# First 62 up-projection units as one 448-column product and one 224-column product

## The chip, the cores and the metric

The kernel runs on one core of one Trainium2 chip. The metric is device time in microseconds, the median of several executions. One execution was also taken with the profiler, and all rows below are of that one.

## The reference, cut to what matters

The reference is a two-layer transformer block over 256 tokens of width 1024: attention and a gated recurrence, then a feed-forward of 16384 experts chosen by keys (PEER), then a second block with a mixer, cross attention and a gated MLP. Everything is fp32. The part that matters here is the expert layer:

```python
sc = jnp.einsum('bshpd,phnd->bshpn', q, keys)     # scores; top 16 of 2 x 128 keys for each of 8 heads
act = jax.nn.gelu(jnp.einsum('tkd,td->tk', ue, ht), approximate=False)   # up-projection of the chosen experts
return jnp.einsum('tk,tkd->td', gt * act, ve)     # gated, down-projection
```

The kernel computes the up-projection of all 16384 experts for 224 of the tokens (the dense part), masks with gates later, and gathers the experts of the other 32 tokens.

## The kernel before, in words

**fp32 in three products.** TensorE's products here are of float32r, so each operand is split into a high part and a low rest: ScalarE makes the high half of a weight unit (`hi`, raw to `whi`), VectorE or GpSimd the low one (`lo`, `wlo = raw - whi`), and `three` adds high x high, high x low and low x high into one PSUM region. A unit is 128 x 1024 weights, 512 KB, fetched by SyncE into 4 `raw` buffers; `whi` and `wlo` have 3 buffers each. The tokens, transposed, stand in `hTh` (high) and `hTl` (low), 8 tiles of 256 columns each.

**The up-projection** (L1075 to L1080) is 128 units, each with 8 steps over k. In one step `lin_T` runs three products of 224 columns, with three weight loads: `whi` on `hTh`, `whi` on `hTl`, `wlo` on `hTh`. Two units share one PSUM bank (224 columns in each half); the banks 4, 5 and 6 go round, the bank being 4 + pair mod 3. After each pair ScalarE applies gelu straight from PSUM into `acts` (L1607 to L1614) and frees the bank.

**Beside it**, in the first 62 units, runs the routing of the tokens (L2045), in two blocks of 128 tokens, nearly all on VectorE. It is a generator of 30 steps. Each engine's program is written by hand: per unit it does its own share and then `side.step`, which runs one step of the routing, or two where `U1_STEPS` (L162) says so: after units 12, 26, 40 and 54. `side.drain` after unit 61 runs what is left. In VectorE's part of a block the steps 1 to 10 are the top 16 of 16 score rows of 128, step 11 casts and adds the candidates, 12 to 21 the top 16 of them, 22 the positions, 23 to 26 comparisons and sums that look up the keys, 27 waits for ScalarE's exponential (its step 22) and normalizes, 28 and 29 are empty, and 30 (L2096 to L2115) waits for three transposes that TensorE makes in its step 30, and copies them out.

**Who makes the low halves.** `on_pool` (L133) gives those that are made in iterations 0 to 51 to GpSimd and the later ones to VectorE. In iteration u an engine prepares unit u + 2. A high half waits until the unit three before it is done on TensorE.

**The gathered tokens.** In iteration 51 VectorE scales one row block (L2124), ScalarE copies it three times in iterations 52 to 54, GpSimd gathers expert rows from iteration 50 on, and VectorE's dot products (L2131) come at iterations 55, 56, 58, 59, 61 and later.

After unit 61 the remaining 66 units run with `lin_T` as well; from unit 70 on the gates are built beside them.

Of the kernel before, what the change touches and what calls it, by code (L numbers as in the profile page):

```python
# [7 lines left out]
ALU = mybir.AluOpType  # L8
# [11 lines left out]
T = 256  # L20
# [14 lines left out]
NG = 32  # L35
# [3 lines left out]
NGRP = TD // OB  # L39
EARLY = 10  # L40
G_DENSE = 70
REP_AT = 51
DOT_AT = [55 + 3 * g // 2 for g in range(EARLY)] + [71 + 2 * (14 * g // 11) for g in range(NPK - EARLY)]
ACC_AT = [57 + 2 * g for g in range(13)] + [97 + 3 * g // 2 for g in range(NPK - 13)]
# [125 lines left out]
hd_pe hd_act hd_dve hd_pool mask xv_ev cr_pe cr_act cr_dve  # L170
ff_a ff_c ff_g ff_h ff_lo
own_act own_dve own_pool zeros x_sq hi_half lo_half lo_first f_xg f_xd f_act hd_mask
pk_idx pk_rep pk_used pk_act
""".split()


# [37 lines left out]
def build(nc, x, mem, wdram, keep_d, con0_d, con1_d, con2_d, keys_d, w2c_d, gf_d, gf2_d,  # L214
          gffn_d, utab, out):
    ctx = ExitStack()
    with ctx:
        def sb(name, n, dt=F32, c=ctx):
            return c.enter_context(nc.sbuf_tensor(name, [P, n], dt))
# [7 lines left out]
        wlo = [sb(f"wlo{i}", UNIT, F32R) for i in range(NSPL)]  # L227
        keep = sb("keep", NKEEP)
        xres = sb("xres", 2048)
        hTh = sb("hTh", 2048, F32R)  # L230
        hTl = sb("hTl", 2048, F32R)
        small = sb("small", 256)
        with ExitStack() as c:
            iT = sb("iT", 3 * T, c=c)
# [6 lines left out]
        row_b = sb("row_b", T, F16)  # L241
        col_b = sb("col_b", T, F16)
        iota_b = sb("iota_b", P * 2, F16)
        zero_b = sb("zero_b", P, BF16)
        first_cut = (sb("first_h", 2 * T, F32R), sb("first_l", 2 * T, F32R))

        with ExitStack() as c:
            A1 = sb("A1", 24576, c=c)
# [23 lines left out]
        def t3(ap, a):  # L272
            return ap.rearrange("p (a b) -> p a b", a=a)

        def t4(ap, a, b):
            return ap.rearrange("p (a b c) -> p a b c", a=a, b=b)
# [18 lines left out]

        K_ = pick(keep, 0, KOFF)
        ident = K_("ident")
        hTv = (t3(hTh[:, :], KD), t3(hTl[:, :], KD))
        xk_end = BASE["w_xk"]

        aqT = t3(a1(0, 1280), 5)
# [64 lines left out]
        acts = t3(A2[:, 0:P * TD], P)  # L366
        hrep = a2(31744, 1024)
        pk_acc = hrep
        pk_idx = small[:, 16:16 + NPK].bitcast(U32)
        pk_gate, pk_dot, pk_co, pk_f = (small[:, o:o + NPK] for o in (48, 80, 112, 144))  # L370

# [8 lines left out]

        def cut(part, n):
            if n < 2:
                return t3(first_cut[part][:, :], 2)[:, n, :]
            return t3((hTh, hTl)[part][:, :], 8)[:, n % 8, :]


        memx = a3(0, 2048)
# [67 lines left out]
        def pe_program(e):  # L455
# [132 lines left out]

            def normed(j):
                return lambda k: e.wait_ge(s["n_lo"], 8 * j + 2 * (k // 2) + 2) if k % 2 == 0 else None  # L590

            def lin_T(u0, units, src, K, first=None, after=None, steps=(1,), c0=0):
                per = KD // K
                for u in range(units):
                    i = u0 + u
                    wv = [z.rearrange("p (n k c) -> p n k c", n=per, k=K) for z in unit(i)]
                    for j in range(per):
                        n = u * per + j
                        q = pair[0]
                        bk = 4 + q % 3  # L600
                        if n % 2 == 0:
                            use(bk)
                        for k in range(K):
                            if n == 0 and first:
                                first(k)
                            ins = three(banks[bk][:, (n % 2) * 256:(n % 2 + 1) * 256 - c0], [z[:, j, k, :] for z in wv],
                                        [z[:, k, c0:T] for z in src], k == 0, k == K - 1)
                            if 2 * (j * K + k + 1) == KD:
                                mid.step()
                        if n % 2:  # L610
                            by, n_ev = PAIR_FREED[q]
                            free[bk] = (s[by], n_ev)
                            pair[0] += 1
                    ins.then_inc(s["w"], 1)
                    if after:
                        after(u)
                    side.step(steps[(i + 1) % len(steps)])
# [455 lines left out]
                    ins.then_inc(s["sc_pe"], 1)  # L1073
                    free[g] = (s["sc_act"], 4 * b + g + 1)
            side.lists[0] += [routing(0), routing(1)]  # L1075
            lin_T(BASE["u"], 62, hTv, KD, steps=U1_STEPS, c0=NG)
            side.drain()
            lin_T(BASE["u"] + 62, G_DENSE - 62, hTv, KD, c0=NG)
            side.lists[0] += [gates(0), gates(1)]
# [107 lines left out]
        def act_program(e):  # L1187
# [57 lines left out]
            def lin_T(u0, units, evict, after=None, per=1, steps=(1,)):  # L1245
                for u in range(units):
                    i = u0 + u
                    hi(i + 2)
                    if (u + 1) * per % 2 == 0:
                        q = pair[0]  # L1250
                        e.wait_ge(s["w"], i + 1)
                        evict((u + 1) * per - 2, t3(banks[4 + q % 3][:, :], 2))
                        pair[0] += 1
                    if after:
                        after(u)
                    side.step(steps[(i + 1) % len(steps)])
# [350 lines left out]
            def gelu(n0):  # L1607
                def f(n, pb):
                    if TD * (n0 + n + 2) > 15872:
                        e.wait_ge(s["rt_dve"], 8)  # L1610
                    if TD * (n0 + n + 2) > 16896:
                        e.wait_ge(s["pk_used"], EARLY)
                    act(acts[:, n0 + n:n0 + n + 2, :], pb[:, :, 0:TD], ACT.Gelu).then_inc(s["ev_act"], 1)
                return f  # L1614
# [5 lines left out]
                    act(hrep[q, :], hrep[0:NG, :], ACT.Copy).then_inc(s["pk_rep"], 1)  # L1620

            side.lists[0] += [routing(0), routing(1)]
            lin_T(BASE["u"], 62, gelu(0), rep_h, steps=U1_STEPS)
            side.drain()
            def first_cuts(u):
                if u == 64:
# [120 lines left out]
        def dve_program(e):  # L1747
# [112 lines left out]
            def lin_T(u0, units, evict=None, before=None, per=1, steps=(1,)):  # L1860
                for u in range(units):
                    i = u0 + u
                    lo(i + 2)
                    if before:
                        before(u)
                    if (u + 1) * per % 2 == 0:
                        q = pair[0]
                        if evict:
                            e.wait_ge(s["w"], i + 1)
                            evict((u + 1) * per - 2, t3(banks[4 + q % 3][:, :], 2))  # L1870
                        pair[0] += 1
                    side.step(steps[(i + 1) % len(steps)])
# [316 lines left out]
            def cut_acts(n):  # L2189
                if n > 127:  # L2190
                    return
                e.wait_ge(s["ca_hi"], n + 1)
                if n == 2:
                    for z in (hTh, hTl):
                        own(e.memset(t3(z[:, :].bitcast(F32), 8)[:, :, 0:NG], 0.0))
                    again()
                tt(cut(1, n)[:, NG:T], acts[:, n, :], cut(0, n)[:, NG:T].bitcast(F32), ALU.subtract
                   ).then_inc(s["ca_lo"], 1)
# [343 lines left out]
            own(e.tensor_copy(banks[7][:, 0:16], K_("iota16")))  # L2542
            own(e.tensor_copy(t3(iota_b[:, :], P), K_("iota").unsqueeze(2).to_broadcast([P, P, 2])))
            side.lists[0] += [routing(0), routing(1)]
            lin_T(BASE["u"], 62, before=pick_u, steps=U1_STEPS)
            side.drain()
            lin_T(BASE["u"] + 62, G_DENSE - 62, before=lambda u: pick_u(u + 62))
            side.lists[0] += [gates(0), gates(1)]
            lin_T(BASE["u"] + G_DENSE, P - G_DENSE, before=lambda u: pick_u(u + G_DENSE))
            for z in first_cut:  # L2550
                own(e.memset(t3(z[:, :].bitcast(F32), 2)[:, :, 0:NG], 0.0))
            again()
            cut_acts(0)
            cut_acts(1)
# [419 lines left out]
```

## Time and profile before

| | us |
|---|---|
| median of 3 runs | 1412.5 |
| range of the runs | 1412.31 to 1413.71 |
| profiled execution | 1412.38 |
| its span on the core | 1410.3 |
| TensorE busy | 1388.3 |
| VectorE busy | 1036.4 |
| ScalarE busy | 735.3 |
| GpSimd busy | 298.3 |

The span runs from the first to the last instruction. The 62 units with the routing beside them lie at 264.4 to about 431 us. In the rows, L466 is TensorE's matmul helper, L1193 ScalarE's and L1761 VectorE's `tensor_tensor`; the tile names tell them apart. Tiles named A are views of the large scratch buffers.

### The profile page before, as it was taken

How to read it: one execution, taken by the hardware profiler on the slowest of the kernel's cores; microseconds unless marked ns; L12 is line 12 of the kernel's file. 1: busy time of each engine (PE TensorE's matmuls, PEld its weight loads, DVE VectorE, ACT ScalarE, POOL GpSimd, SP SyncE). 2: the span in 40 equal slices, each digit the busy share in tenths (PEclk: the TensorE clock that was granted, in tenths of full speed). 3: DMA queues.
4: the chain of work that ended last, by engine and by line, in shares of the span. 5: the costliest groups of instructions: out<-in, count | busy, mean ns of one | idle time of the engine just before them, and what ended most of it. 6: DMA issues, size and time to landing. Idle time of an engine off the chain costs nothing.

```text
span 1410.3 us, 25136 instructions
## 1 busy us (share of the span) xinstructions
PE 1388.3 (98%) x10156; PEld 1255.5 (89%) x10157; DVE 1036.4 (73%) x1841; ACT 735.3 (52%) x1070; POOL 298.3 (21%) x176
## 2 busy tenths in 40 slices
PE   9999999999999999999999999999999999999997
PEld 7989989999999999997777788888899798899985
DVE  5665574694987999998888777688777755777754
ACT  5674655545464444444444445544567654655543
POOL 5000000488862222210000031144213000000000
PEclk9999999999999999999999999999999999999999
DMA  6433356455679777765555588788443553555552
GB/s 242 150 127 127 130 170 225 149 195 195 194 250 342 242 250 251 253 219 168 178 168 170 190 294 286 262 300 316 151 150 119 165 165 105 179 180 185 189 192 92
DMA packets 76579, 279.16 MB, mean 198 GB/s; under 512 B 8496, under 2 KB 8752, under 8 KB 76208
## 3 DMA queue, kind: packets, MB, share of 16 engines
q1 hardware_dynamic: 67104, 243.73, 51.3%
q0 software_dynamic: 9216, 33.56, 6.3%
q8 instruction: 81, 1.33, 0.4%
q14 instruction: 34, 0.28, 0.1%
q10 hardware_dynamic: 144, 0.26, 0.0%
HBM read 276.47 MB, written 1.05 MB: 197 GB/s over the span
## 4 chain that ended last, share of the span: by engine, by line
PE 75%; issue 15%; ACT 4%; DVE 4%; POOL 1%; DMA 0%; SPq 0%; POOLq 0%; DVEq 0%; ACTq 0%
PE bank L466 74%; ACT A L1193 2%; ACT whi L1193 2%; DVE wlo L1761 1%; POOL wlo L2653 1%; PE bank L475 1%; ACT L1193 1%; DVE A L1761 1%; DVE A L1757 0%; DMA raw<-in_w_in_t 0%; DVE xres L1761 0%; ACT hTh L1193 0%; DVE small L2453 0%; DVE small L1761 0%; POOL small L2659 0%
## 5 line engine op out<-in xcount | busy, mean ns | idle before, releaser
L1193 ACT ACTIVATE whi<-raw 128x1024 fp32r<-128x1024 f32 (+1 forms) x450 | 473.3, 1054 | 390.0 <-PE bank L466 388.1
L1761 DVE TENSOR_TENSOR wlo<-raw,whi 128x1024 fp32r<-128x1024 f32 (+1 forms) x385 | 472.0, 1227 | 258.5 <-ACT whi L1193 255.9
L466 PE MATMUL bank<-hTh,whi 128*128 128x224 f32 (+1 forms) x1944 | 547.7, 282 | 2.6 <-DVE wlo L1761 1.7
L466 PE MATMUL bank<-hTh,wlo 128*128 128x224 f32 (+1 forms) x1944 | 540.1, 278 | 0.0
L466 PE MATMUL bank<-hTl,whi 128*128 128x224 f32 (+1 forms) x1944 | 540.0, 278 | 0.0
L466 PEld LDWEIGHTS bank<-hTh,whi 128*128 128x128 f32 x1944 | 370.0, 190 | 6.7 <-DVE wlo L1761 2.5
L466 PEld LDWEIGHTS bank<-hTl,whi 128*128 128x128 f32 x1944 | 370.0, 190 | 0.3 <-issue 0.2
L466 PEld LDWEIGHTS bank<-hTh,wlo 128*128 128x128 f32 x1944 | 369.9, 190 | 0.0
L466 PE MATMUL bank<-whi,hTh 128*128 128x512 f32 (+2 forms) x552 | 217.4, 394 | 0.2 <-DVE wlo L1761 0.2
L466 PE MATMUL bank<-whi,hTl 128*128 128x512 f32 (+2 forms) x552 | 214.2, 388 | 0.0
L466 PE MATMUL bank<-wlo,hTh 128*128 128x512 f32 (+2 forms) x552 | 214.2, 388 | 0.0
L1193 ACT ACTIVATE A<-bank 128x512 f32<-128x512 f32 (+3 forms) x163 | 87.4, 543 | 209.7 <-PE bank L466 200.1
L2653 POOL TENSOR_TENSOR wlo<-raw,whi 128x1024 fp32r<-128x1024 f32 x63 | 150.7, 2411 | 135.1 <-ACT whi L1193 132.6
L466 PEld LDWEIGHTS bank<-whi,hTh 128*128 128x128 f32 x552 | 103.6, 188 | 24.0 <-issue 0.8
L466 PEld LDWEIGHTS bank<-whi,hTl 128*128 128x128 f32 x552 | 103.5, 188 | 23.8
L466 PEld LDWEIGHTS bank<-wlo,hTh 128*128 128x128 f32 x552 | 103.7, 188 | 22.3
L2669 POOL DMA_INDIRECT A<-in_v,small x32 | 56.7, 1772 | 301.5 <-DVE A L1757 188.4
L2659 POOL TENSOR_TENSOR small<-small 128x1 f32<-128x1 f32 x16 | 9.6, 598 | 513.8 <-DVE small L1758 510.0
L2669 POOL DMA_INDIRECT A<-in_utab,small x32 | 53.7, 1678 | 133.3 <-DVE A L1764 131.8
L466 PE MATMUL bank<-A 128*128 128x128 f32 (+9 forms) x472 | 69.9, 305 | 0.1
L466 PEld LDWEIGHTS bank<-A 128*128 128x128 f32 (+4 forms) x472 | 59.4, 182 | 6.5 <-issue 2.5
L1761 DVE TENSOR_TENSOR hTl<-A,hTh 128x224 fp32r<-128x224 f32 x126 | 48.5, 385 | 0.0
(192 smaller groups left out, 1550.4 us busy)
## 6 DMA issues: line engine op xcount, KB each, us to landing
raw<-in_u SPq DMA_DIRECT2D x128, 512.0 KB, 3.3
raw<-in_v SPq DMA_DIRECT2D x128, 512.0 KB, 3.3
raw<-in_w_up SPq DMA_DIRECT2D x44, 512.0 KB, 3.3
raw<-in_w_down SPq DMA_DIRECT2D x22, 512.0 KB, 3.3
raw<-in_w_in_t SPq DMA_DIRECT2D x17, 512.0 KB, 4.1
raw<-in_w_in_g SPq DMA_DIRECT2D x16, 512.0 KB, 3.2
raw<-in_w_out SPq DMA_DIRECT2D x16, 512.0 KB, 3.9
raw<-in_w_pq SPq DMA_DIRECT2D x16, 512.0 KB, 4.4
```

Of the source, the lines that this page charges most:

```text
L466: return e.matmul(o, l, r, start=st, stop=sp_, skip_group_check=True)
L475: return e.transpose(o, i, ident[0:k, 0:k])
L1193: return e.activation(o, i, func, **kw)
L1761: return e.tensor_tensor(o, a, b, op)
L2653: e.tensor_tensor(l, raw[i % NRAW][:, :], h.bitcast(F32), ALU.subtract).then_inc(s["lo_pool"], 1)
L2659: e.tensor_tensor(st[:, 2:3], st[:, 3:4], mhalf, ALU.pow).then_inc(s["n_rstd"], 1)
L2669: e.indirect_dma_start(out=pk_buf(g), out_offset=None, in_=table, in_offset=bass.IndirectOffsetOnAxis(ap=pk_idx[:, i:i + 1], axis=0)).then ...
```

## The change

The first 62 units (`WIDE`) run in a new function `wide`. The high and low tokens now lie in one tile `hT`, so that `whi` is loaded once for each k and multiplied with high and low tokens in one product of 448 columns; `wlo` on the high tokens is a product of 224 columns into the first half. A unit fills a bank alone: the first 224 columns hold high x high plus low x high, the second 224 high x low. ScalarE copies the second half to a buffer (`take_b`), VectorE adds the first half to it into `acts` (`add_b`), which frees the bank, and ScalarE applies gelu in place in `acts` for two units at a time, one iteration later (`gelu_wide`). In the order of the programs, ScalarE's copy comes after the high half of the iteration, and VectorE's add before the routing step. The buffers `u_b` are three, two of them in `og`, which is unused until the gates.

```diff
+            def wide(units, steps):
+                both = t4(hT[:, :], 2, KD)
+                for u in range(units):
+                    i = BASE["u"] + u
+                    wv = two(unit(i), KD)
+                    bk = 4 + u % 3
+                    use(bk)
+                    for k in range(KD):
+                        mm(banks[bk][:, 0:2 * TD], wv[0][:, k, :], both[:, :, k, NG:T], k == 0, False)
+                        ins = mm(banks[bk][:, 0:TD], wv[1][:, k, :], both[:, 0, k, NG:T], False, k == KD - 1)
+                        if 2 * (k + 1) == KD:
+                            mid.step()
+                    ins.then_inc(s["w"], 1)
+                    free[bk] = (s["u_sum"], u + 1)
+                    if u % 2:
+                        pair[0] += 1
+                    side.step(steps[(i + 1) % len(steps)])
...
-            lin_T(BASE["u"], 62, hTv, KD, steps=U1_STEPS, c0=NG)
+            wide(WIDE, U1_STEPS)
...
-            lin_T(BASE["u"], 62, gelu(0), rep_h, steps=U1_STEPS)
+            def take_b(n):
+                if n >= 3:
+                    e.wait_ge(s["u_sum"], n - 2)
+                e.wait_ge(s["w"], BASE["u"] + n + 1)
+                act(u_b[n % 3], banks[4 + n % 3][:, TD:2 * TD], ACT.Copy).then_inc(s["u_b"], 1)
+
+            def gelu_wide(n):
+                if TD * (n + 2) > 15872:
+                    e.wait_ge(s["rt_dve"], 8)
+                e.wait_ge(s["u_sum"], n + 2)
+                z = acts[:, n:n + 2, :]
+                act(z, z, ACT.Gelu).then_inc(s["ev_act"], 1)
+
+            for u in range(WIDE):
+                i = BASE["u"] + u
+                hi(i + 2)
+                if u:
+                    take_b(u - 1)
+                rep_h(u)
+                if u % 2 and u > 1:
+                    gelu_wide(u - 3)
+                    pair[0] += 1
+                side.step(U1_STEPS[(i + 1) % len(U1_STEPS)])
+            take_b(WIDE - 1)
+            gelu_wide(WIDE - 2)
+            pair[0] += 1
             side.drain()
...
-            lin_T(BASE["u"], 62, before=pick_u, steps=U1_STEPS)
+            def add_b(n):
+                e.wait_ge(s["u_b"], n + 1)
+                if TD * (n + 1) > 15872:
+                    e.wait_ge(s["rt_dve"], 8)
+                tt(acts[:, n, :], banks[4 + n % 3][:, 0:TD], u_b[n % 3], ALU.add).then_inc(s["u_sum"], 1)
+
+            for u in range(WIDE):
+                i = BASE["u"] + u
+                lo(i + 2)
+                if u:
+                    add_b(u - 1)
+                pick_u(u)
+                if u % 2:
+                    pair[0] += 1
+                side.step(U1_STEPS[(i + 1) % len(U1_STEPS)])
             side.drain()
+            add_b(WIDE - 1)
```

The rest of the diff declares `hT` with its two halves, the buffer `u_b2`, one tile for the two `first_cut` halves, and the semaphores `u_b` and `u_sum`.

## Rows read from the trace of the kernel before

**Rows 1.** The page, first part: busy time of each engine, its share of the span

```profile
PE 1388.3 (98%) x10156; PEld 1255.5 (89%) x10157; DVE 1036.4 (73%) x1841; ACT 735.3 (52%) x1070; POOL 298.3 (21%) x176
```

**Rows 2.** TensorE's waits from 264 to 432 us: who waited for whom, us, times, longest

```profile
PE bank L466 <- POOL wlo L2653: 0.2, 1, 0.2
```

**Rows 3.** Busy time by engine from 264.4 to 430.4 us

```profile
core 0: us, PE busy (x) PEld busy (x) DVE busy (x) ACT busy (x) POOL busy (x), PEclk, DMA share, GB/s
264.40:430.40 166.00, 165.81 (x1486) 165.63 (x1485) 137.14 (x480) 89.34 (x103) 133.66 (x59) 1.00 0.61 207
```

**Rows 4.** Timeline of ScalarE: start us, us, engine, line, operation, idle before and releaser

```profile
240.49 0.60 ACT L1193 ACTIVATE A<-bank 128x512 f32<-128x512 f32 x1 [1.72 <-PE bank L466]
...
257.53 0.60 ACT L1193 ACTIVATE A<-bank 128x512 f32<-128x512 f32 x1 [1.72 <-PE bank L466]
...
302.19 0.55 ACT L1193 ACTIVATE A<-bank 128x448 f32<-128x448 f32 x1 [1.56 <-PE bank L466]
302.63 1.05 ACT L1193 ACTIVATE whi<-raw 128x1024 fp32r<-128x1024 f32 x1
...
318.26 0.55 ACT L1193 ACTIVATE A<-bank 128x448 f32<-128x448 f32 x1 [1.56 <-PE bank L466]
```

**Rows 5.** Timeline of TensorE in the down-projection

```profile
640.11 0.39 PE L466 MATMUL bank<-whi,hTl 128*128 128x512 f32 x1
...
643.61 0.40 PE L466 MATMUL bank<-whi,hTl 128*128 128x512 f32 x1
```

**Rows 6.** Timeline of VectorE, first block's routing

```profile
265.30 3.19 DVE L2017 MAX8 A<-A 128x8 f32<-128x128 f32 x16 [7.96 <-ACT A L1193]
...
284.54 0.32 DVE L2051 CAST A<-A 128x256 f32<-128x256 uint32 x1
...
303.81 2.48 DVE L1761 TENSOR_TENSOR bank<-A,bank 128x512 f32<-128x512 f32 x4
...
311.16 2.49 DVE L1761 TENSOR_TENSOR bank<-A,bank 128x512 f32<-128x512 f32 x4
...
340.03 0.56 DVE L2097 COPY iT<-bank 128x384 f32<-128x384 f32 x1 [17.67 <-PE bank L475]
...
341.42 2.39 DVE L1761 TENSOR_TENSOR gate<-iT,gate 128x128 f16<-128x128 f32 x1
...
344.03 2.30 DVE L1764 SCALAR_TENSOR_TENSOR small<-A 32x32 f32<-32x32 f32 x1
...
347.07 2.31 DVE L2115 CAST small<-small 128x32 uint32<-128x32 f32 x1
349.30 3.18 DVE L2017 MAX8 A<-A 128x8 f32<-128x128 f32 x16
```

**Rows 7.** Timeline of VectorE, end of the second block's routing

```profile
397.14 1.54 DVE L1764 SCALAR_TENSOR_TENSOR A<-xres,small,A 32x1024 f32<-32x1024 f32 x1
...
405.87 2.34 DVE L1761 TENSOR_TENSOR wlo<-raw,whi 128x1024 fp32r<-128x1024 f32 x1 [2.28 <-ACT whi L1193]
...
416.21 1.22 DVE L1764 SCALAR_TENSOR_TENSOR A<-A 128x1024 f32<-128x1024 f32 x1
417.36 0.08 DVE L1764 DVE_READ_ACCUMULATOR A<-A 128x1 f32 x1
...
418.74 0.29 DVE L1761 TENSOR_TENSOR gate<-iT,gate 128x128 f16<-128x128 f32 x1
```

**Rows 8.** Groups by shape, 340 to 420 us: count, busy us, mean ns; last from the page

```profile
L2653 POOL TENSOR_TENSOR wlo<-raw,whi 128x1024 fp32r<-128x1024 f32 x25 | 60.3, 2429 | 7.2 <-ACT whi L1193 7.2
...
L1761 DVE TENSOR_TENSOR bank<-A,bank 128x512 f32<-128x512 f32 x8 | 5.0, 684 | 0.0
...
L1193 ACT ACT_TABLE_LOAD x2 | 2.6, 1283 | 0.0
...
L2051 DVE CAST A<-A 128x256 f32<-128x256 uint32 x1 | 2.4, 2395 | 0.0
...
L1761 DVE TENSOR_TENSOR hTl<-A,hTh 128x224 fp32r<-128x224 f32 x126 | 48.5, 385 | 0.0
```

More of the change, by code:

```diff
@@ L41 @@
 G_DENSE = 70
+WIDE = 62
 REP_AT = 51
@@ L172 @@
 own_act own_dve own_pool zeros x_sq hi_half lo_half lo_first f_xg f_xd f_act hd_mask
-pk_idx pk_rep pk_used pk_act
+u_b u_sum pk_idx pk_rep pk_used pk_act
 """.split()
@@ L229, in build @@
         xres = sb("xres", 2048)
-        hTh = sb("hTh", 2048, F32R)
-        hTl = sb("hTl", 2048, F32R)
+        hT = sb("hT", 4096, F32R)
+        hTh, hTl = hT[:, 0:2048], hT[:, 2048:4096]
         small = sb("small", 256)
@@ L243, in build @@
         iota_b = sb("iota_b", P * 2, F16)
+        u_b2 = sb("u_b2", 2 * TD, F16)
         zero_b = sb("zero_b", P, BF16)
-        first_cut = (sb("first_h", 2 * T, F32R), sb("first_l", 2 * T, F32R))
+        first_both = sb("first_cut", 4 * T, F32R)
+        first_cut = (first_both[:, 0:2 * T], first_both[:, 2 * T:4 * T])
         with ExitStack() as c:
@@ L297, in build @@
         ident = K_("ident")
-        hTv = (t3(hTh[:, :], KD), t3(hTl[:, :], KD))
+        hTv = (t3(hTh, KD), t3(hTl, KD))
         xk_end = BASE["w_xk"]
@@ L368, in build @@
         pk_acc = hrep
+        u_b = [z.bitcast(F32) for z in (og[:, 0:2 * TD], og[:, 2 * TD:4 * TD], u_b2[:, 0:2 * TD])]
         pk_idx = small[:, 16:16 + NPK].bitcast(U32)
@@ L382, in cut @@
             if n < 2:
-                return t3(first_cut[part][:, :], 2)[:, n, :]
-            return t3((hTh, hTl)[part][:, :], 8)[:, n % 8, :]
+                return t3(first_cut[part], 2)[:, n, :]
+            return t3((hTh, hTl)[part], 8)[:, n % 8, :]
         memx = a3(0, 2048)
@@ L2194, in cut_acts @@
                     for z in (hTh, hTl):
-                        own(e.memset(t3(z[:, :].bitcast(F32), 8)[:, :, 0:NG], 0.0))
+                        own(e.memset(t3(z.bitcast(F32), 8)[:, :, 0:NG], 0.0))
                     again()
@@ L2550, in dve_program @@
             for z in first_cut:
-                own(e.memset(t3(z[:, :].bitcast(F32), 2)[:, :, 0:NG], 0.0))
+                own(e.memset(t3(z.bitcast(F32), 2)[:, :, 0:NG], 0.0))
             again()
```

## Prediction

> **What bounds the kernel now.** I read the page first: TensorE is busy for 98% of the span [rows 1]. That alone doesn't say it is at its peak, so the second view is who TensorE waited for in the first 62 units of the up-projection, the only place where the arithmetic changes: 0.2 us in all [rows 2]. The third view is that stretch by engine [rows 3]: the granted clock is 1.00, so 2.4 GHz; VectorE is busy for 137.1 of 166.0 us and GpSimd for 133.7. TensorE sets the pace, but the two engines behind it have little room. The rest of the kernel is left alone, and what this stretch gains or loses moves all behind it, since TensorE has hardly an idle stretch there either. So the question has two halves: how much shorter is a unit on TensorE, and can the others keep up.
>
> **A unit on TensorE.** ScalarE's gelus, one for two units, start at 302.19 and 318.26: 16.07 us for 6 units, 2.68 us each [rows 4], 24 products of 224 columns, 111.6 ns each. The new unit has 8 products of 448 columns and 8 of 224. No row shows 448 columns. The 256-column products before (17.04 us from 240.49 to 257.53 for 6 units of 24) take 118.3 ns each [rows 4], and 15 products of 512 columns take 3.50 us, 233.3 ns each [rows 5]. The line through both is 0.449 ns a column: 204.6 ns at 448, and 103.9 at 224, where 111.6 is measured. So something other than columns holds the 224-column product, and I keep 111.6 for it. A unit P is 8 x (204.6 + 111.6) = **2.53 us**, 0.149 less than now, 9.2 us in 62 units. From below: 448/2.4 = 186.7, plus the 11.6 that the 256-column product has over its columns, 198.3, and 103.9 for the other: 2.42 us, 16 us less. From above: the wide product costs as much as the two it replaces, 2.68 us, no gain. I take the line, since its 512-column end is nearest to 448.
>
> The Trainium skill (TensorE: Matmul & The Clock Gate, section LDWEIGHTS) gives a weight load of 128 columns as columns/1.2, 107 ns, which would be what holds the 224-column product at 111.6; that agrees with the row and says the narrow half stays there. Its section Back-to-back issue gap gives N/2.4 + 2.5 ns, 189 ns at 448; the trace disagrees at 512 (233 against 216). By it P would be 2.41, about the lower end above.
>
> **The copies.** ScalarE copies 224 columns from PSUM, 62 times. 512 columns take 0.60 and 448 0.55 [rows 4], so 0.37 us by that slope. Its gelu reads SBUF instead. Per pair of units it then has 2 x 1.06 (the high halves) + 0.74 + 0.55 = 3.4 us of 5.06: room enough.
>
> **The adds.** VectorE gets 62 adds of 224 columns, one input in PSUM. A 224-column tensor_tensor takes 0.385, a 512-column one 0.684, but four with a PSUM operand in a row take 2.48, so 0.62 each [rows 6, 8]: 0.30 less for 288 fewer columns is 0.32; I take **0.35** with the wait's handling. Bounds 0.32 and 0.45. 62 x 0.35 = 21.7 us onto 137.1 makes 159 of 62 x 2.53 = 157 us. VectorE is then full. Worse, it is now tied on both sides: an add can't start before its unit is done, and TensorE can't start unit u+3 in the same bank before add(u). Before, a bank held two units and VectorE could run far ahead (it stood 17.67 us waiting for TensorE [rows 6]).
>
> **How late may an add be.** After the end E of unit u, ScalarE reacts 0.29 us later (unit 13 ends at 264.4 + 14 x 2.68 = 301.9, gelu at 302.19 [rows 3, 4]), makes the high half first (1.06), then the copy (0.37), VectorE adds (0.385), some 0.1 for two handovers: E + 2.2. TensorE wants the bank two units later, E + 5.06. So VectorE may lag by **2.9 us**; any more stops TensorE. Queued behind the add on VectorE is its routing step; behind ScalarE's copy and gelu are its next high halves, and GpSimd's low halves behind those.
>
> **Routing steps against the lag.** One step runs after each unit, two after units 12, 26, 40 and 54. From the order in the code, step 23 of the first block comes in iteration 21, step 30 in 27, steps 53 and 60 (the second block's 23 and 30) in 49 and 55.
> - Iterations 0 to 20. Steps 1 to 10 take 19.2 us (265.30 to 284.54), steps 11 to 22 19.3 (284.54 to 303.81), of which 2.9 for step 11 alone [rows 6]: 1.9 and 1.6 on average, with the add under P. No stall; VectorE idles, the time isn't banked.
> - Iterations 21 to 24. Steps 23 and 24 take 5.0 and 2.35 us, and again for 25 and 26 (7.35 from 303.81 to 311.16, twice) [rows 6]. With adds 5.35, 2.7, 5.35, 2.7 against 2.53 each: 16.1 - 10.1 = 6.0 late, less 2.9: TensorE stops **3.1 us**.
> - Iteration 27. Step 30 waits for TensorE's transposes after unit 27: 340.03 is 0.6 after the unit's end at 264.4 + 28 x 2.68 = 339.4 (E + 0.64). It took 9.27 us (340.03 to 349.30) [rows 6]. Three small instructions in it took 2.39, 2.30 and 2.31; the first takes 0.29 when GpSimd is idle [rows 7], so about 6.3 of it are waits for GpSimd, whose subtractions take 2.4 us each [rows 8]. GpSimd will be fuller than now (2.43 us in units of 2.53), so I keep the 9.27. Add(27) ends at E + 10.3, TensorE wants it two units later, plus half of the 0.64 for the transposes, E + 5.4: **4.9 us**.
> - Iterations 28 to 48. Steps 1 to 10 with adds 22.7 of 25.3 us, which wears the lag off, as steps 12 to 22 do in ten units; the second block's cast of 2.395 [rows 8] makes step 11 about 5: 0.1 us of stall.
> - Iterations 49 to 52: 5.35, 2.65, then 5.0 + 1.5 for the gather row [rows 7] + 0.35, then 2.3 + 0.35 + the low half that VectorE now takes over (1.15, as the dot product of the same size, 416.21 to 417.36; 2.34 beside GpSimd [rows 7]): 19.3 - 10.1 - 2.9 = 6.2 us. Iteration 55 has low half, dot product (1.15), step 60 (1.7 with GpSimd idle, 417.36 to 419.03 [rows 7]) and add: 0.7 more. **6.9 us**.
> - After unit 61 the next unit takes bank 4 + 64 mod 3 = 5, the bank of unit 61 itself. It waits for copy and add: 0.29 + 0.37 + 0.385 + 0.05 = **1.1 us**.
>
> **Sum.** -9.2 + 3.1 + 4.9 + 0.1 + 6.9 + 1.1 = +6.9 us. On the profiled execution's 1412.38 us (span 1410.3, 2.1 around it; median of the runs 1412.5) that is **1419 us**. The renamed tiles and the merged buffers cost nothing: same instructions, same bytes.
>
> **Rivals.**
> - Quick product and free port (faster). The mechanism: P is 2.42, and GpSimd's idle moments fall so that VectorE's small instructions don't meet its subtractions. Gain 16.2; stalls with a lag of 2.6: 3.7, 0, 0, 6.6, 1.1 = 11.4. Net -4.8: 1407.6. For it: the second tail had no such waits; against: GpSimd was idle by then. It decides only if both hold; with P 2.42 and the port waits kept the stalls are 3.7, 5.1, 1.3, 7.7, 1.1, net +2.7: 1415. Chance 0.15.
> - Free port alone, P 2.53: stalls 3.1, 0, 0, 5.8, 1.1 = 10.0, net +0.8: 1413. Chance 0.15.
> - The wide product saves nothing (P 2.68). The change then doesn't do what it says. Lag 3.2: stalls 2.1, 4.6, 0, 5.8, 1.1 = 13.6, net near 13: 1426. Against: rows 5 show no penalty for long products. Chance 0.1.
> - ScalarE in the loop. A late add holds ScalarE's gelu, the next high half comes late, GpSimd, with 0.1 us of room in a unit, can't catch up, and TensorE waits for low halves as well. It bites where two table loads of 1.28 us [rows 8] and an exponential hold ScalarE, in iterations 20 and 48, and beside the two gathers at 50 and 51: some 4 us more, 1423. Chance 0.15.
> - The forecast, 1419 +- 3: chance 0.45.
>
> **Range and chances.** 0.2% of 1412.5 is 2.8 us, about what a measurement of this kernel can tell from no change. Faster, below 1409.7: the first rival and a little of the second, 0.18. Same, to 1415.3: most of the second and the low edge of the forecast, 0.16. Slower: 0.66. The range, 1409 to 1426, leaves out the first rival's low end and what lies over the third's.
>
> **What would show it.** Right: pitch of the wide product near 205 ns and of the narrow near 112 where TensorE runs free; units of 2.53 us up to unit 20; TensorE waits for the adds at about units 24 to 26, 30, 52 to 55 and 62; VectorE nearly full from unit 21 on; the stretch some 7 us longer. Wrong: a first routing tail of 3 us instead of 9, or units of 2.4 us; then the time falls toward 1413 or below. Waits of TensorE for GpSimd's low halves would speak for ScalarE in the loop. An add of over 0.5 us would raise every stall of VectorE's alike.

## The result, and the profile after

The changed kernel takes 1427.4 us (median of 4 runs, 1425.5 to 1430.9) against 1412.4, a ratio of 1.0107 (95% interval 1.0086 to 1.0128). It is 15.0 us slower. The forecast was slower, 1419 us, range 1409 to 1426: the sign was right, the time lies outside the range. The profiled execution took 1428.06 us with a span of 1426.0.

First, the busy times on the page of the kernel after. They answer to [rows 1]: TensorE is busy for the same time as before in a longer span, VectorE for 21.4 us more, as 62 adds of 0.35 should.

```profile
PE 1389.1 (97%) x9661; PEld 1245.2 (87%) x9661; DVE 1057.8 (74%) x1903; ACT 751.0 (53%) x1132; POOL 298.1 (21%) x176
```

Second, who TensorE waited for, the view of [rows 2]. 0.2 us have become 15.6, 14.0 of them for VectorE's add into `acts` (A).

```profile
PE bank L470 <- DVE A L1808: 14.0, 6, 4.7
PE bank L470 <- POOL wlo L2715: 1.6, 3, 0.6
```

Third, the price of a unit. In ScalarE's timeline two high halves stand 6 units apart: 15.36 us, 2.56 us a unit (the column after the start is the duration). In TensorE's, a pair of wide and narrow product takes 0.32 us (299.84 to 300.80 for three), the wide one 0.22 and the narrow one 0.10 of it.

```profile
298.50 1.06 ACT L1215 ACTIVATE whi<-raw 128x1024 fp32r<-128x1024 f32 x1 [1.25 <-PE bank L470]
...
313.86 1.06 ACT L1215 ACTIVATE whi<-raw 128x1024 fp32r<-128x1024 f32 x1 [1.26 <-PE bank L470]
```

```profile
299.84 0.38 PE L470 MATMUL bank<-hT,whi 128*128 128x448 f32 x1
300.06 0.27 PE L470 MATMUL bank<-hT,wlo 128*128 128x224 f32 x1
300.16 0.38 PE L470 MATMUL bank<-hT,whi 128*128 128x448 f32 x1
...
300.80 0.38 PE L470 MATMUL bank<-hT,whi 128*128 128x448 f32 x1
```

Fourth, the large stops in TensorE's timeline, in brackets the idle time before the instruction and who ended it. Counting units from 0 by their products, they lie before units 26, 30, 54 and 62.

```profile
335.71 0.44 PE L470 MATMUL bank<-hT,whi 128*128 128x448 f32 x1 [2.38 <-DVE A L1808]
...
349.11 0.44 PE L470 MATMUL bank<-hT,whi 128*128 128x448 f32 x1 [2.64 <-DVE A L1808]
...
418.01 0.71 PE L470 MATMUL bank<-hT,whi 128*128 128x448 f32 x1 [4.72 <-DVE A L1808]
...
444.13 0.74 PE L470 MATMUL bank<-hT,whi 128*128 128x224 f32 x2 [2.83 <-DVE A L1808]
```

Fifth, the granted clock (the column before the last two) in slices of 5 us. It is 1.00 until the stop of 4.7 us. During that stop it falls to 0.50, 1.2 GHz, and it is back at 1.00 some 5 us after TensorE has gone on. The same happens in the stop of 2.8 us, with some 6 us at the half clock behind it. The stops of 2.4 and 2.6 us did not do that in this execution.

```profile
core 0: us, PE busy (x) PEld busy (x) DVE busy (x) ACT busy (x) POOL busy (x), PEclk, DMA share, GB/s
410.00:415.00 5.00, 2.81 (x16) 2.40 (x16) 4.97 (x7) 3.40 (x4) 3.13 (x3) 1.00 0.73 248
415.00:420.00 5.00, 1.99 (x7) 1.90 (x8) 5.00 (x7) 2.09 (x5) 0.00 (x0) 0.62 0.68 229
420.00:425.00 5.00, 5.00 (x24) 4.68 (x24) 4.42 (x9) 2.51 (x4) 0.00 (x0) 0.70 0.45 145
425.00:430.00 5.00, 5.00 (x34) 4.71 (x34) 4.90 (x13) 2.68 (x5) 0.94 (x1) 1.00 0.79 239
440.00:445.00 5.00, 2.17 (x13) 1.85 (x12) 2.97 (x5) 2.92 (x6) 0.94 (x1) 0.85 1.03 415
445.00:450.00 5.00, 5.00 (x25) 5.00 (x25) 2.37 (x3) 0.88 (x2) 0.94 (x1) 0.50 0.78 247
```

Added up, from unit 0 to the clock's return: -7.4 (62 x 0.119) + 17.1 (nine stops: 15.6, and 0.17 each in which the products' modelled ends hide the idle time) + 2.1 (8 pairs of products at 0.587 instead of 0.320 us) + 2.8 (27 narrow products at 0.214 instead of 0.112 us) = 14.6. Unit 0 itself begins 0.5 us later than before. Of the 15.7 us between the spans, 0.6 are not in this account; some 0.3 of them are the units behind a stop, which take 2.60 to 2.61 instead of 2.56 us. The account also shows where the loss lies: unit 28 begins 76.2 us after unit 0, against 75.4 before, and unit 66 begins 116.8 us after unit 28, against 102.7 before.

Last, the same stretch before and after by engine, cut at the end of the first routing block's tail (349 us).

```profile
core 0: us, PE busy (x) PEld busy (x) DVE busy (x) ACT busy (x) POOL busy (x), PEclk, DMA share, GB/s
264.40:349.00 84.60, 84.60 (x761) 84.60 (x760) 62.26 (x235) 44.78 (x52) 73.42 (x31) 1.00 0.56 187
349.00:431.00 82.00, 81.81 (x733) 81.63 (x732) 75.48 (x246) 44.56 (x52) 60.24 (x29) 1.00 0.68 229
```

```profile
264.40:349.00 84.60, 78.48 (x490) 72.86 (x488) 73.36 (x264) 49.95 (x79) 71.69 (x30) 1.00 0.59 182
349.00:444.00 95.00, 85.65 (x515) 79.13 (x515) 87.36 (x281) 55.82 (x88) 62.68 (x30) 0.96 0.66 214
```

This is the view that the prediction should have had: before, VectorE has 22.3 us idle in the first part, of which 17.67 are one wait for transposes [rows 6], and only 6.5 us in the second.

### The profile page after: what moved, and what is told of

It is laid out like the page before. It is cut to its first block, busy times and chain, and to the rows that moved or that the text cites. A ratio compares the mean times of both kernels' runs of the same rounds, so it can differ in the third digit from the quotient of the medians.

```text
span 1426.0 us, 24359 instructions
## 1 busy us (share of the span) xinstructions
PE 1389.1 (97%) x9661; PEld 1245.2 (87%) x9661; DVE 1057.8 (74%) x1903; ACT 751.0 (53%) x1132; POOL 298.1 (21%) x176
## 4 chain that ended last, share of the span: by engine, by line
PE 71%; issue 15%; DVE 8%; ACT 4%; DMA 1%; POOL 1%; SPq 0%; POOLq 0%; ACTq 0%; DVEq 0%
PE bank L470 70%; DVE A L1808 2%; DVE wlo L1808 2%; ACT A L1215 2%; ACT whi L1215 2%; PE bank L479 1%; DVE A L1804 1%; ACT L1215 1%; DVE bank L1808 1%; DMA raw<-in_u 1%; DVE A L1811 0%; DMA raw<-in_w_in_t 0%; DVE xres L1808 0%; POOL wlo L2715 0%; DVE A L2132 0%
## 5 line engine op out<-in xcount | busy, mean ns | idle before, releaser
L470 PE MATMUL bank<-hT,whi 128*128 128x256 f32 (+2 forms) x3392 | 679.9, 298 | 18.1 <-DVE A L1808 14.0
L470 PEld LDWEIGHTS bank<-hT,whi 128*128 128x128 f32 x3392 | 540.0, 191 | 34.3 <-issue 10.1
L470 PE MATMUL bank<-hT,wlo 128*128 128x224 f32 (+1 forms) x1944 | 538.1, 277 | 0.0
L470 PEld LDWEIGHTS bank<-hT,wlo 128*128 128x128 f32 x1944 | 372.9, 192 | 0.0
L470 PE MATMUL bank<-whi,hT 128*128 128x512 f32 (+2 forms) x1104 | 346.5, 391 | 0.2 <-DVE wlo L1808 0.2
L470 PEld LDWEIGHTS bank<-whi,hT 128*128 128x128 f32 x1104 | 205.3, 188 | 47.5 <-issue 0.8
L470 PE MATMUL bank<-wlo,hT 128*128 128x512 f32 (+2 forms) x552 | 214.5, 389 | 0.0
L1215 ACT ACTIVATE A<-bank 128x512 f32<-128x512 f32 (+2 forms) x132 | 70.4, 542 | 166.6 <-PE bank L470 157.0
L470 PEld LDWEIGHTS bank<-wlo,hT 128*128 128x128 f32 x552 | 103.9, 188 | 22.2
L1808 DVE TENSOR_TENSOR hT<-A,hT 128x224 fp32r<-128x224 f32 x126 | 48.6, 386 | 0.0
```

What stands on the lines that cost most here:

```text
L470: return e.matmul(o, l, r, start=st, stop=sp_, skip_group_check=True)
L1215: return e.activation(o, i, func, **kw)
L1808: return e.tensor_tensor(o, a, b, op)
```

## The experiments

Their times stand beside runs of the kernel before on the same chip (medians 1412.2 to 1412.5). One caution on profiled executions: in unchanged code between 165 and 207 us an execution loses 0 to 2.5 us more than another (unit 0 starts between 264.4 and 266.9 us); the medians hold, a single span must be read less that start.

**1. Three narrow products in the new structure.** The two halves of a bank are now two sums, each with its own start, and the sum in the bank does not come out right. Why was not looked into; the run is for the time alone.

```diff
-                        mm(banks[bk][:, 0:2 * TD], wv[0][:, k, :], both[:, :, k, NG:T], k == 0, False)
+                        mm(banks[bk][:, 0:TD], wv[0][:, k, :], both[:, 0, k, NG:T], k == 0, False)
+                        mm(banks[bk][:, TD:2 * TD], wv[0][:, k, :], both[:, 1, k, NG:T], k == 0, k == KD - 1)
```

> The changed kernel with its new structure (a bank for each unit, ScalarE's copy, VectorE's add), but three products of 224 columns as before instead of the wide one. Theory (the time goes into TensorE's stops for late adds, and into the half clock behind the long ones): units of 2.68 us instead of 2.56 give back 7.4 us, a lag of 3.2 instead of 2.9 takes some 3 us off the stops: 1426 to 1431 us, with stops near units 23, 25, 30, 52 to 54 and 62. Rival (the wide product or its two-piece operand is what costs): the time falls back to within 3 us of 1412.4.

Measured: 1431.6 us (ratio 1.0138, 1.0121 to 1.0155), a little above the expected range. The stops are 11.8 us for adds and 0.8 for low halves. So the structure costs 19.4 us, and going from three narrow products to the wide one takes 4.2 us off, not the 7.4 of its units. The wide product itself is not what costs.

**2. The adds alone in the kernel before.**

```diff
+            def pick_and_add(u):
+                if u:
+                    again()
+                    own(tt(t3(extra[:, :], 14), banks[7][:, 0:16].unsqueeze(1).to_broadcast([P, 14, 16]),
+                           t3(extra[:, :], 14), ALU.add))
+                pick_u(u)
-            lin_T(BASE["u"], 62, before=pick_u, steps=U1_STEPS)
+            lin_T(BASE["u"], 62, before=pick_and_add, steps=U1_STEPS)
```

> The kernel before with 61 additional adds of 224 columns on VectorE in the same places of its program, one operand in PSUM, on a buffer of their own that nobody waits for (their result is not used). Theory (it is the coupling, not VectorE's load): VectorE had 29 us idle in the stretch, the adds take 20 to 24, so 1412 to 1415 us. Rival (VectorE has too little time for the adds): 1418 us or more, with TensorE waiting for VectorE's low halves from unit 54 on.

Measured: 1420.5 us (1.0056, 1.0039 to 1.0072). **My theory fell here, the rival holds.** No one waits for these adds, and they cost 8.2 us. In the profiled execution unit 0 began 1.65 us late; the rest is one stop of 4.2 us before unit 54, whose low half is the first that VectorE makes, and the half clock behind it.

```profile
415.64 0.55 PE L467 MATMUL bank<-hTh,whi 128*128 128x224 f32 x1 [4.20 <-DVE wlo L1762]
...
415.00:420.00 5.00, 4.36 (x20) 4.36 (x21) 4.93 (x7) 0.39 (x1) 0.00 (x0) 0.50 0.39 138
```

The same by blocks, from the start of the second routing block on VectorE to 0.7 us before unit 62 (first line before, second with the adds; the columns are those of the view above):

```profile
349.30:431.00 81.70, 81.51 (x730) 81.33 (x729) 75.18 (x246) 44.37 (x51) 59.94 (x29) 1.00 0.68 229
350.95:439.34 88.39, 84.19 (x730) 83.95 (x729) 85.37 (x279) 44.23 (x51) 60.30 (x29) 0.96 0.64 213
```

33 adds fall in it, and VectorE is busy for 10.2 us more. Its idle time falls from 6.5 to 3.0 us, and the other 6.7 us make the block longer. Not all of that is bare arithmetic: the product that scales the gathered rows took 1.54 us before [rows 7] and 3.98 here, beside a subtraction of GpSimd's (406.05 to 408.46 us). It lies on the path to the low half that TensorE stops for. Whether the adds would cost less if that instruction did not meet the subtraction was not tried.

```profile
405.56 3.98 DVE L1765 SCALAR_TENSOR_TENSOR A<-xres,small,A 32x1024 f32<-32x1024 f32 x1
```

**3. The last bank.** Bank 4 + (u + 2) mod 3 for unit u instead of 4 + u mod 3, in the programs of all three engines (TensorE's line is shown):

```diff
-                    bk = 4 + u % 3
+                    bk = 4 + (u + 2) % 3
```

> The changed kernel with the bank order moved by two, so that unit 62 does not take the bank of unit 61 but that of unit 59. Theory: the stop of 3.0 us before unit 62 and the half clock behind it (27 products at 214 instead of 112 ns, 2.8 us) go: 1421 to 1423 us, and no granted clock under 1.00 between 440 and 450 us. Rival (VectorE and the late raw unit hold unit 63 or 64 anyway, the stop only moves): 1425 to 1427 us.

Measured: 1424.4 us (1.0079, 1.0062 to 1.0096), 3.0 less than the change where 5.8 were expected, and between the theory's range and the rival's. The stop before unit 62 is gone, and the clock is 1.00 from 440 to 450 us. In this execution it fell behind the stop of 2.4 us at 336 us instead (0.66 from 335 to 340), which it had not done before: whether a stop of that size costs the clock differs from run to run.

**4. Five banks.** Banks 2 and 3 beside 4, 5 and 6, five copy buffers, gelu two pairs later, the routing's masks in SBUF (the last is not shown):

```diff
+WB = (2, 3, 5, 6, 4)
...
-                    bk = 4 + u % 3
+                    bk = WB[u % 5]
...
-                if n >= 3:
-                    e.wait_ge(s["u_sum"], n - 2)
+                if n >= 5:
+                    e.wait_ge(s["u_sum"], n - 4)
...
-                if u % 2 and u > 1:
-                    gelu_wide(u - 3)
+                if u % 2 and u > 5:
+                    gelu_wide(u - 7)
```

> The changed kernel with five banks and five copy buffers for the wide units instead of three, and gelu two pairs later on ScalarE. The two banks come from the routing, whose comparison masks go to SBUF and whose index values go to a PSUM bank that it already has, so that each of its instructions still has one SBUF input. Lag allowed: 2.9 + 2 x 2.56 = 8 us. Theory (only the short lag is at fault): all stops go, 62 units at 2.56 give 7.4 us less than before, 1405 to 1407 us, granted clock 1.00 throughout the stretch. Rival (VectorE is full: 159 us of work in 62 x 2.56 = 159): stops stay at the end of the second routing block, 1409 to 1413 us.

Measured: 1417.6 us (1.0038, 1.0024 to 1.0052), above both expectations. All waits for adds are gone. What is left are 2.6 us in five waits for GpSimd's low halves, 1.5 us in which the transposes before unit 28 wait for the routing's values from VectorE, and a stop of 4.3 us for a low half of VectorE's:

```profile
413.15 0.74 PE L472 MATMUL bank<-hT,whi 128*128 128x448 f32 x1 [4.32 <-DVE wlo L1811]
```

```profile
411.88 1.22 DVE L1811 TENSOR_TENSOR wlo<-raw,whi 128x1024 fp32r<-128x1024 f32 x1
```

It is unit 54's. VectorE starts it as soon as its comparisons are through; they stand before it in its program. Five banks take 9.8 us of the loss away, not the rest.

**5. No adds at all.** ScalarE copies both halves and frees the bank; the high x low part is left out of the sum.

```diff
-                    free[bk] = (s["u_sum"], u + 1)
+                    free[bk] = (s["u_b"], u + 1)
...
+                act(u_b[n % 3], banks[4 + (n + 2) % 3][:, TD:2 * TD], ACT.Copy)
+                act(acts[:, n, :], banks[4 + (n + 2) % 3][:, 0:TD], ACT.Copy).then_inc(s["u_b"], 1)
...
-                if u:
-                    add_b(u - 1)
```

> The wide products as in the change, with the bank order of the run with the moved end, but without VectorE: ScalarE copies both halves out (two copies of 224 columns a unit, then gelu in place), which frees the bank, and nobody adds the halves, so the sum lacks its high x low part. This prices the wide product by itself. Theory (the product is worth 62 x 0.12 = 7.4 us and VectorE's share takes it away): 1405 to 1407 us, no stop of TensorE over 1 us. Rival (something else of the new form costs too, ScalarE's order or GpSimd's room of 0.1 us in a unit): 1409 us or more, with stops for GpSimd's low halves.

Measured: 1410.7 us (0.9984, 0.9975 to 0.9994): without VectorE's share the wide form is worth some 2 us in this kernel, not 7.4. The rival holds. There is a **second limit** behind VectorE: three stops for GpSimd's low halves, before units 51 to 53, and some 3 us of half clock behind the last one.

```profile
PE bank L470 <- POOL wlo L2705: 3.2, 3, 2.0
```

```profile
394.19 2.39 POOL L2705 TENSOR_TENSOR wlo<-raw,whi 128x1024 fp32r<-128x1024 f32 x1 [2.29 <-ACT whi L1215]
397.52 2.40 POOL L2705 TENSOR_TENSOR wlo<-raw,whi 128x1024 fp32r<-128x1024 f32 x1 [0.94 <-ACT whi L1215]
400.10 2.23 POOL L2721 DMA_INDIRECT A<-in_utab,small  x1 [0.17 <-issue]
402.36 2.37 POOL L2705 TENSOR_TENSOR wlo<-raw,whi 128x1024 fp32r<-128x1024 f32 x1
```

GpSimd waits 2.29 and 0.94 us for high halves, since ScalarE loads two tables and computes the exponential there, and then a gather of 2.23 us stands between two subtractions of 2.4. At 2.56 us a unit, TensorE would be there some 6 us earlier than before. One thing was not taken apart: ScalarE makes a second copy of 0.35 us per unit here, which can make its high halves later by itself.

**6. Adds two units later.**

```diff
-                if u:
-                    add_b(u - 1)
+                add_to(u if u in (27, 55) else u - 2)
```

> The five-bank kernel with VectorE's adds two units later, so that VectorE may also run up to 5 us ahead of TensorE (in iterations 27 and 55, where it waits for the transposes anyway, it adds all that is there). In the five-bank kernel the whole stop of 4.3 us was for unit 54's low half, the first one that VectorE makes, and VectorE had idled 17 us in the units before. Theory (it is the tie from below, add not before the unit's end, that keeps VectorE from working ahead): the stop of 4.3 and the half clock behind it (10 pairs of products, 2.7 us) go, 1409 to 1411 us by that, and less if the small stops go too. Rival (VectorE is full): the stop moves to a unit between 54 and 62, 1414 to 1418 us.

Measured: 1417.8 us (1.0034, 1.0022 to 1.0046), unchanged against experiment 4. The stop before unit 54 is gone (0.9 us are left before unit 55), but one of 4.9 us appeared before unit 32: I had let the add of unit 27 wait for iteration 30, behind the tail and two steps. By itself this run tells little; the first kernel of experiments 11 and 12 (below) repeats it without that mistake.

**7. The first 18 units only.** Three banks, `WIDE = 18`, the other 44 units as before.

```diff
-WIDE = 62
+WIDE = 18
...
+            lin_T(BASE["u"] + WIDE, 62 - WIDE, hTv, KD, steps=U1_STEPS, c0=NG)
```

> The change for the first 18 units only, the other 44 of the stretch as before: all of it lies in VectorE's light routing steps and before its 17.67 us of waiting. Theory: 18 x 0.12 = 2.1 us gained and no stop, 1410 to 1411 us. Rival (the wide form costs something at its start or end that the stops have hidden): 1412.5 us or more.

Measured: 1412.3 us (0.9997, 0.9988 to 1.0006), no difference; the expected 1410 to 1411 was missed. The waits show 0.7 us of stops for GpSimd's low halves, before units 23 and 53, 1.0 with what the modelled ends hide. So half of the 2.1 us is lost; the other half is less than these runs can tell from nothing.

**8. The clock by itself.** In the five-bank kernel:

```diff
+                    if u == 54:
+                        spin(18, 1)
                     wv = two(unit(i), KD)
```

> The five-bank kernel with 18 products of zeros (bf16, 512 columns, some 3.9 us) into an idle bank on TensorE just ahead of unit 54, where it stands for 4.3 us. Nothing else changes, the stop stays. Theory (after the stop TensorE runs at the half clock, 1.2 GHz, for ten pairs of products, 0.587 instead of 0.320 us each): the granted clock stays at 1.00 and 2.7 us go, 1414.5 to 1415.5 us. Rival (the low clock in the records costs nothing by itself): 1417 to 1418 us, as without.

Measured: 1417.4 us (1.0031, 1.0019 to 1.0042) against 1417.6 without. The clock did stay up:

```profile
408.71 4.06 PE L472 MATMUL bank<-zero_b 128*128 128x512 bf16 x18
413.19 0.47 PE L472 MATMUL bank<-hT,whi 128*128 128x448 f32 x1 [0.42 <-DVE wlo L1813]
```

```profile
410.00:415.00 5.00, 4.58 (x24) 2.81 (x23) 5.00 (x7) 3.41 (x5) 0.00 (x0) 1.00 0.69 224
415.00:420.00 5.00, 4.18 (x28) 3.69 (x27) 4.93 (x9) 2.06 (x4) 0.00 (x0) 1.00 0.53 182
```

and yet hardly anything was won. Counted from unit 0, TensorE is 1.7 us earlier at unit 62 than in experiment 4 and only 0.5 us at unit 66: it stood 0.8 and 0.9 us more for VectorE's low halves, before units 55 and 64. **Here the half clock costs next to nothing, since another engine sets the pace behind it.** By the same argument the first 2.1 us of my account above, behind the stop before unit 54, would lie within VectorE's time in the change too; that was not tried in the kernel with three banks.

**9. Wide for the first 28 units** (five banks, late adds; `WIDE = 28`, the adds of 26 and 27 while VectorE waits for the transposes anyway).

```diff
-WIDE = 62
+WIDE = 28
...
+                add_to(u + 1 if u == WIDE - 1 else u - 2)
...
+            lin_T(BASE["u"] + WIDE, 62 - WIDE, hTv, KD, steps=U1_STEPS, c0=NG)
```

> Five banks and adds that may lie two units back, as in the kernel with late adds, but the wide form for the first 28 units only, so that it ends with the first routing block; units 28 to 61 as before. The adds of units 26 and 27 come while VectorE waits for the transposes. Theory (VectorE's spare time lies in the first block, 17.67 us in which it waited for TensorE's transposes, and almost none in the second): 28 x 0.12 = 3.3 us earlier transposes, and all behind them as before, 1409 to 1410 us. Rival (ScalarE and GpSimd, not VectorE, have no room, as in the kernel without adds): stops for GpSimd's low halves from unit 20 on, 1411.5 us or more.

Measured: 1410.3 us, ratio 0.9986 (0.9977 to 0.9995): 2.0 us less than before, just above the expected 1409 to 1410, and nothing of the reference is left out. One stop is left in the whole stretch, and VectorE is busy for 78.1 of the first 84.6 us, where it had 62.3:

```profile
PE bank L472 <- POOL wlo L2732: 0.4, 1, 0.4
```

```profile
264.40:349.00 84.60, 84.60 (x565) 80.02 (x564) 78.06 (x265) 53.97 (x82) 76.52 (x32) 1.00 0.60 193
349.00:431.00 82.00, 81.59 (x731) 81.41 (x731) 77.08 (x247) 44.33 (x51) 58.45 (x28) 1.00 0.72 239
```

**10. Wide for the last 34 units** (the change's form, from unit 28 on, bank 4 + (u + 1) mod 3).

```diff
+            lin_T(BASE["u"], W0, hTv, KD, steps=U1_STEPS, c0=NG)
...
-                for u in range(units):
+                for u in range(W0, units):
```

> The change for units 28 to 61 only, units 0 to 27 as before (three banks, one order moved so that the banks join). Theory: VectorE's second block has some 6 us to spare and gets 34 x 0.37 = 12.6 us of adds, so nearly the whole loss of 15 us is here: 1421 to 1427 us. Rival (the loss is spread over the stretch, per unit): 34/62 of 15 us, 1420 us or less.

Measured: 1426.7 us (1.0101, 1.0086 to 1.0117): nearly the whole loss with 34 of 62 units. In part this agreement is luck: the first tail took 11.5 us here (340.49 to 351.95) against 7.2 in the change, since four of its small instructions met GpSimd's subtractions, and TensorE stopped for 5.9 us before unit 31. But the change's own trace says the same: there the first 28 units lose 0.9 us and the stretch from unit 28 to 66 loses 14.1.

**11 and 12. All 62 units with room in banks and order, with and without relief for VectorE.** Adds up to two units back, caught up behind the tails; in the one called relief the index searches of the second block are left out.

```diff
+                add_to(u if 27 <= u < 39 or u > 52 else u - 2)
...
+                    if find:
                         e.max_index(idxs[:, j, 0:8], vals[:, j, 0:8], src[:, j, :])
```

> The same kernel with the searches kept, to compare. Theory: VectorE's second block sets the end. The adds alone cost 8.2 us there, the transposes come 28 x 0.12 = 3.3 us earlier, so 1412.5 + 4.9 = 1417.4 us, whatever banks, order of adds or clock do; 1416 to 1418.5. Rival (the stop of 4.9 us at unit 32 in the kernel with late adds was a loss by itself): it goes, and the time falls to 1413 us or below.

> All 62 units wide, five banks, adds that lie two units back, except after each block's tail (units 27 to 38, and from 53), where all that is ready is added at once; and VectorE's index searches of the second routing block left out, 14.9 us of its work (the second 128 tokens then use the first ones' indices). Theory (VectorE's work in the second block is the limit): 1405 to 1408 us, stops under 2 us in sum. Rival (ScalarE's and GpSimd's chain is the limit as soon as units take 2.56 us): 1410 us or more, as without adds.

Measured: 1418.2 us (1.0041, 1.0025 to 1.0056) with the searches, 1411.2 us (0.9990, 0.9981 to 1.0000) without. Five banks in three orders (experiments 4, 6, 8 and 11) all come to 1417.4 to 1418.2, which is what VectorE's account gives: 8.2 for the adds less 3.3 for the earlier transposes. That account was made after the first three of these times were known, so only the fourth tests it. With the searches a stop of 4.7 us before unit 54 stays, now for an add, and the product of 32x1024 takes 3.84 us again. Taking 14.9 us of work off VectorE's second block gives 7.0 us and no more. The time is the rival's, but its mechanism is only a part: of the stops that are left, 1.4 us are for GpSimd's low half beside its gather, 2.7 are for adds (1.8 before unit 32, behind the first block's tail) and 1.3 for a low half of VectorE's before unit 64.

```profile
PE bank L472 <- DVE A L1811: 2.7, 2, 1.8
PE bank L472 <- POOL wlo L2726: 1.4, 1, 1.4
PE bank L472 <- DVE wlo L1811: 1.3, 1, 1.3
```

## Why the prediction was right and wrong, point by point

**The steps that failed.** The stops of TensorE were forecast at 16.1 us in all and stand at 17.1 in the profiled execution, so that list was nearly right in sum, since a tail priced too high stood against an end priced too low. What failed were three terms: the unit was priced at 2.53 us and took 2.56 (1.8 us in 62 units), the stop before unit 62 was priced at 1.1 us and took 3.0, and the clock behind the stops was put at nothing, where products at half speed take 4.9 us more. Beneath that lies a step of the mechanism: VectorE's room was counted over all 62 units together, while only 6.5 us of it lie in the second block.

- **A unit on TensorE: a term mis-sized.** Forecast 2.53, measured 2.56; the gain 7.4 us instead of 9.2. The pair costs 0.320 instead of 0.316, and the split differs: 0.22 for the wide product and 0.10 for the narrow one, against 204.6 and 111.6 ns. An estimate from the Trainium skill (TensorE: Matmul & The Clock Gate, section Back-to-back issue gap, whose formula is for a product by itself, and section LDWEIGHTS) makes the pair 189 + 107 = 296 ns; the trace disagrees with both parts, with 220 for the wide product and 100, under the load's 107, for the narrow one behind it.
- **The adds and the copies: right.** An add lasts 0.38 us, and the instruction behind it starts 0.30 us after it (409.04 and 409.34 us in VectorE's timeline); a copy lasts 0.34.
- **Stops at units 24 to 26: right.** Forecast 3.1; 0.72 and 2.38, 3.4 with the hidden idle time. Before unit 23 stands a wait of 0.49 for GpSimd's low half that the sum had not.
- **The first tail, unit 30: right in mechanism, too large.** Forecast 4.9, measured 2.8. It met GpSimd's subtractions twice, not three times, and took 7.2 us instead of 9.27 (341.41 to 348.58); how often it meets them differs between kernels, as the 11.5 us of experiment 10 show. The rival of the free port didn't occur.
- **Units 52 to 55: right in place and nearly in size, in part by luck.** Forecast 6.9, all of it for VectorE. Measured 0.70 and 4.72 for adds, 5.8 with the hidden time; 0.62 and 0.49 for GpSimd's low halves, before units 53 and 51, bring it to 7.2, and they are the mechanism of a rival. The forecast's own terms, with the low half at 1.15 us as written, add up to 18.65 and not to 19.3, which makes some 6.3 instead of 6.9.
- **Before unit 62: the step was right, its size wrong.** Forecast 1.1, measured 3.0. The high half of unit 63 waited 2.35 us for its weights (it starts at 439.92), and copy and adds stood behind it in ScalarE's and VectorE's order. I had priced the chain with all its neighbours on time.
- **The clock: a term that the sum lacked.** I named a stop of 4.9 us and never asked what the clock does behind it. In the trace the products at half speed take 4.9 us more than at full speed, 2.1 behind the stop before unit 54 and 2.8 behind that before unit 62. Experiment 8 shows, with five banks, that this is not a plain addend: before unit 54 it costs next to nothing, since VectorE sets the pace. What it costs behind unit 62, where VectorE has room, was not tried apart from the stop; both together were 3.0 us less in experiment 3, where the clock fell elsewhere.
- **What the sum couldn't see.** The prediction did count VectorE as full, 159 of 157 us, but spread over 62 units, and then summed TensorE's stops one by one. Experiments 2, 9 and 10 show the better account: two blocks, the first with 22 us to spare, most of it a wait for the transposes, the second with 6.5. And it took the stops for a matter of lag alone. Two more banks cure 9.8 of the 15.0 us. The other 5.2 are VectorE's work in the second block, by experiments 2 and 12, with a part for GpSimd's and ScalarE's chain that no run takes apart.
- **The rivals.** By its time the nearest was the wide product that saves nothing, at 1426, but its mechanism is refuted: a unit takes 2.56 us, and three narrow products in its place cost 4.2 us more (experiment 1). ScalarE in the loop, at 1423, is in the trace with its mechanism (1.6 us of waits for low halves, and 3.2 in experiment 5), but the larger part of the miss is the end at unit 62 and the clock. The three sizes that fell short (1.8 for the unit, 1.9 at the end, up to 4.9 for the clock) less the 2.1 too many at the tail make 6.5 of the 8.4 us between forecast and result, if the clock is counted in full. That a range up to 1426 was missed by only 1.4 us owes something to errors of opposite sign, the tail above all.

**What stays open.** Why the fetch for unit 63 came late in that one execution and how often it does, what the clock costs behind unit 62 alone, how much of the cost on VectorE is its meetings with GpSimd, and 0.6 us of the account.

## What to carry to other kernels

An engine's idle time is no reserve unless it lies where the new work must be done: cut the stretch at the points where the engine waits for others, and compare new work and idle time block by block. When a result needs a second engine before its buffer is free, a helper engine that used to run ahead becomes part of the pace; more buffers gave back 9.8 of 15.0 us here, what was lost to unevenness, and not what was lost to work. Half of a change can be worth more than all of it: here the first 28 units alone gain 2 us (with five banks), the other 34 alone lose 14.

## What the runs showed of the hardware

- A wide float32r product of 448 columns and a narrow one of 224, each with its weight load, take 0.320 us together, against 3 x 0.112 = 0.335 us for three narrow ones. For the same columns, two weight loads instead of three save only 4.5% of the time.
- The granted clock fell from 2.4 to 1.2 GHz in every stop of 4.2 to 5.9 us (the change and experiments 1 to 4, 6, 10 and 11), in one of 2.8 us in the change, with stops of 2.4 and 2.1 us in experiments 3 and 1, and some 1.5 us behind one of 2.0 in experiment 5. Stops of 2.4 and 2.6 us in the change and of 2.3 and 2.7 in experiments 1 and 3 left it at 1.00. At the half clock the pair of products takes 0.587 instead of 0.320 us.
- Keeping TensorE busy with products of zeros through a stop of 4.3 us held the clock at 1.00 (experiment 8).
- A cast of 128x128 on VectorE that takes 0.23 us by itself took 2.29 in the first tail of the change, beside GpSimd's subtraction of 128x1024; the product of 32x1024 took 1.28 us in experiment 6, 2.17 in the change and 3.98 in experiment 2.
